# Attention probabilities divided before the transpose and used as the moving operand, pool weights folded into the output weights, and weight loads reordered

## The reference

```python
p = rmsnorm(h) @ w_in                         # q (8 heads x 64) | k, v (2 x 64) | u (512)
q, k = rope(q), rope(k)                       # first 16 dims of a head
s = q @ k.T / 8                               # keys: own and previous block of 128, masked to a window of 128
m = max(max(s), sink); e = exp(s - m)
a = (e / (sum(e) + exp(sink - m))) @ v
d[g] = windowed mean of u[g] - u[g]           # windows 2, 4, 8, 16; g = 0..3, 128 channels each
pm[g] = (d[g] @ pool_w[g]) * pool_scale[g]
h = h + concat(a, pm) @ w_out                 # 1024 x 1024
h = h + square(relu(rmsnorm(h) @ w_up)) @ w_down   # 1024 x 4096, 4096 x 1024
```

## Time and profile before

| | us |
|---|---|
| median of three runs (3076.12 to 3078.6) | 3076.51 |
| the profiled execution | 3078.81 |
| its span on the slowest core (core 7) | 3077.0 |
| spans of the eight cores | 3055.1 to 3077.0 |
| PE busy | 2822.4 |
| DVE, ACT, POOL busy | 1559.5, 1525.0, 181.1 |

### The profile page before, as it was taken

The page is one execution under the profiler, slowest core; times in us unless marked ns, Lnnn a source line. Parts: engine busy times, 40 slices in busy tenths (PEclk is TensorE's granted clock), DMA queues, the critical chain, the costliest instruction groups (busy, mean ns, idle before and its releaser), DMA issues.

```text
span 3077.0 us, 52361 instructions; the slowest of 8 cores (3055.1 to 3077.0 us)
## 1 busy us (share of the span) xinstructions
PE 2822.4 (92%) x17326; PEld 1462.9 (48%) x17326; DVE 1559.5 (51%) x3239; ACT 1525.0 (50%) x3827; POOL 181.1 (6%) x318
## 2 busy tenths in 40 slices
PE   1667899999999999999996777999999999999998
PEld 0334455545455555554453333545554554545445
DVE  1334454555465555554452444555556555555544
ACT  1434554545454555554552335555555555555544
POOL 0010000000000000000000100000000000000001
PEclk9888999999999999999998888999999999999999
DMA  9598125262534234245539972243433334242437
GB/s 200 110 191 200 61 91 178 97 193 97 162 123 144 111 125 150 98 172 146 165 113 196 205 175 81 85 166 109 141 122 110 151 108 164 86 165 103 159 112 246
DMA packets 105118, 431.69 MB, mean 140 GB/s; under 512 B 18700, under 2 KB 37100, under 8 KB 67896
## 3 DMA queue, kind: packets, MB, share of 16 engines
q0 software_dynamic: 76192, 314.30, 35.9%
q1 hardware_dynamic: 28664, 114.05, 10.8%
HBM read 404.04 MB, written 74.51 MB: 156 GB/s over the span
## 4 chain that ended last, share of the span: by engine, by line
PE 84%; DMA 9%; SPq 2%; issue 2%; DVE 2%; ACT 2%; DVEq 0%; ACTq 0%; POOLq 0%; POOL 0%
PE ps_all L1036 28%; PE ps_all L1054 28%; PE ps_all L588 10%; PE ps_all L978 7%; DMA s_wup<-w_up 3%; PE ps_all L548 2%; SPq L432 2%; PE ps_all L748 2%; PE ps_all L790 2%; DMA s_wdn<-dn_bf 2%; DMA s_wdn<-w_dn 1%; DMA s_h<-meta 1%; PE ps_all L749 1%; PE ps_all L750 1%; DVE s_xhat L541 1%
## 5 line engine op out<-in xcount | busy, mean ns | idle before, releaser
L1036 PE MATMUL ps_all<-s_xn2T,s_wup 128*128 128x512 bf16 (+2 forms) x4608 | 1029.9, 370 | 52.0 <-DMA s_wup<-w_up 41.0
L1054 PE MATMUL ps_all<-s_wdn,s_aT 128*128 128x512 bf16 x4288 | 1045.3, 382 | 21.8 <-DMA s_wdn<-w_dn 9.2
L1058 DVE TENSOR_TENSOR s_h<-s_h,ps_all 128x512 f32<-128x512 f32 x1072 | 735.4, 686 | 615.0 <-PE ps_all L1054 587.2
L1036 PEld LDWEIGHTS ps_all<-s_xn2T,s_wup 128*128 128x128 bf16 x4608 | 450.4, 99 | 514.7 <-issue 74.3
L1040 ACT ACTIVATE s_relu<-ps_all 128x512 f32<-128x512 f32 (+2 forms) x576 | 324.8, 567 | 674.2 <-PE ps_all L1036 672.6
L1054 PEld LDWEIGHTS ps_all<-s_wdn,s_aT 128*128 128x128 bf16 x4288 | 402.2, 98 | 452.5 <-issue 57.9
L1041 ACT ACTIVATE s_aT<-s_relu 128x512 bf16<-128x512 f32 (+2 forms) x576 | 344.5, 602 | 34.7 <-PE ps_all L1054 5.6
L588 PE MATMUL ps_all<-s_win,s_xnT 128*128 128x512 bf16 (+1 forms) x1632 | 315.5, 350 | 8.3 <-DVE s_xnT L553 5.7
L772 ACT ACTIVATE s_P<-ps_all,s_stat 128x256 bf16<-128x256 f32 x520 | 239.8, 478 | 117.0 <-DVE s_stat L762 116.0
L978 PE MATMUL ps_all<-s_wout,s_mixT 128*128 128x512 bf16 x1072 | 250.7, 385 | 1.9 <-ACT s_mixT L825 1.2
L588 PEld LDWEIGHTS ps_all<-s_win,s_xnT 128*128 128x128 bf16 x1632 | 161.2, 99 | 162.8 <-issue 22.2
(11 more groups left out here) (122 smaller groups left out, 2089.1 us busy)
## 6 DMA issues: line engine op xcount, KB each, us to landing
s_wup<-up_bf POOLq DMA_DIRECT2D x128, 1024.0 KB, 5.5
s_wdn<-dn_bf POOLq DMA_DIRECT2D x128, 1024.0 KB, 6.4
h_mid<-s_h SPq DMA_DIRECT2D x34, 512.0 KB, 6.8
s_h<-h_mid SPq DMA_DIRECT2D x34, 512.0 KB, 7.4
s_wup<-w_up POOLq DMA_DIRECT2D x16, 1024.0 KB, 28.0
s_wdn<-w_dn POOLq DMA_DIRECT2D x16, 1024.0 KB, 29.4
s_h<-x_p SPq DMA_DIRECT2D x32, 512.0 KB, 7.7
up_bf<-s_wup SPq DMA_DIRECT2D x16, 1024.0 KB, 10.2
```

Of the source, the lines that this page charges most:

```text
L1036: r = e.matmul(ps_t[bk][:, 0:n], lhsT=wup_t[s][:, k, fc * 128:(fc + 1) * 128], rhs=x2[:, k, 0:n], start=(k == 0), stop=(k == 7))
L1054: r = e.matmul(ps_t[db][:], lhsT=aT[:, fc, j * 128:(j + 1) * 128], rhs=wdn_t[s][:, fc, hf * 512:(hf + 1) * 512], start=(fc == 0), stop=(fc ...
L1058: dve(lambda e, hf=hf, db=db: e.tensor_tensor(out=h_t[hs][:, hf * 512:(hf + 1) * 512], in0=h_t[hs][:, hf * 512:(hf + 1) * 512], in1=ps_t[d ...
```

## The change

It has five parts.

1. P is multiplied by the reciprocals on DVE before its transpose. PV takes v as weights (64 columns) and P transposed as the moving operand (512 columns), the two kv heads in the two column halves of the array. The result is already transposed, so that the division, the transposes L822 and the small copies go.
2. `poolW` goes. Once per layer pool_w (given transposed) is scaled by pool_scale and multiplied into the lower half of w_out.
3. The sample tile moves from the second to the fourth group of each layer; its two kv halves are built side by side in one PSUM bank each, with two buffers for kc and vc.
4. Layer 0's groups 0 and 1 both read w_up and w_down as f32; the write-back is in group 1. In groups 2 to 6, after every second piece, one DRAM-to-DRAM cast on POOL prepares layer 1's weights (w_in, w_out, 16 pieces), which are then read as bf16 only.
5. At the start the first two tiles' rows go ahead of other loads, and masks, bmat, scales, sinks and the second gains wait for the first transposes, some x loads for those of an earlier tile. The planner gets one rate per queue. One relu buffer instead of two.

```diff
 MACROS = [
-    [[0, 1], [33, 2, 3, 4]] + [list(range(a, a + 4)) for a in range(5, 33, 4)],
+    [[0, 1], [2, 3, 4, 5], [6, 7, 8, 9], [10, 33, 11, 12]] + [list(range(a, a + 4)) for a in range(13, 33, 4)],
...
-DMA_BW = 300e3
+DMA_BW = {"pool": 330e3, "sp": 200e3, "act": 200e3}
...
-    r_t, r_b = sbn("relu", 2, [128, 512])
+    r_t, r_b = sbn("relu", 1, [128, 512])
...
     def load_x(l, ti, hs):
+        early = [first_pe[-2]] if l == 0 and 2 <= len(first_pe) < 8 else []
...
     def load_att_weights(l):
...
+            dma("pool", win_t[:].rearrange("p k n -> p (k n)"), win_d, reads=[win_db], writes=[win_b], sembuf=win_b)
...
+    converts = [(win_d.rearrange("p (k n) -> p k n", k=8), w_in[1].rearrange("(k p) n -> p k n", p=128), win_db),
+                (wout_d.rearrange("p (k n) -> p k n", k=8), w_out[1].rearrange("(k p) n -> p k n", p=128), wout_db)]
+    for p_ in range(NPIECE):
+        converts.append((up_d[1, p_].rearrange("p (k n) -> p k n", k=8), up_src(1, p_), up_db[1][p_]))
+        converts.append((dn_d[1, p_].rearrange("p (c n) -> p c n", c=4), dn_src(1, p_), dn_db[1][p_]))
+    def convert_next():
...
+        last = len(S.ops) - 1
+        while S.ops[last].eng != "pe":
+            last -= 1
+        out, in_, db = converts[i]
+        dma("pool", out, in_, writes=[db, cvt_b[i % 2]], sembuf=cvt_b[i % 2], after=[last])
...
-        if m == 0:
-            dma("pool", wup_t[s][:], w_up[l][:, p * 512:(p + 1) * 512].rearrange("(k p) n -> p k n", p=128),
-                writes=[wup_b[s]], sembuf=wup_b[s])
-            dma("sp", up_d[l, p], flat, reads=[wup_b[s]], writes=[up_db[l][p]], sembuf=wst_b[0][s])
+        if l == 0 and m < 2:
+            dma("pool", wup_t[s][:], up_src(l, p), writes=[wup_b[s]], sembuf=wup_b[s])
+            if m == 1:
+                dma("sp", up_d[l, p], flat, reads=[wup_b[s]], writes=[up_db[l][p]], sembuf=wst_b[0][s])
...
+    def fold_pool(l):
+        for g in range(4):
+            dve(lambda e, g=g: e.tensor_scalar(out=pw_t[:, g, :], in0=pw_t[:, g, :], scalar1=pscale_t[:, l * 4 + g:l * 4 + g + 1], scalar2=None, op0=ALU.mult),
+                [pw_b, pscale_b], [], pw=[fold_b[g]], cost=0.15)
...
+                for hf in range(2):
+                    r = e.matmul(ps_t[bk[hf]][:], lhsT=pw_t[:, g, :], rhs=wout_t[:, 4 + g, hf * 512:(hf + 1) * 512], start=True, stop=True)
...
+    def load_rest():
+        dma("sp", masks_t[:], masks_d, writes=[masks_b], after=[first_pe[0]], sembuf=masks_b)
...
-        act(lambda e: e.activation(out=d_t[:].rearrange("p g t -> p (g t)"), in_=ps_t[bdT][:], func=AF.Copy), [ps_b[bdT]], [d_b], cost=0.6)
-
-        def poolW(e):
...
+        act(lambda e: e.activation(out=mix[:, 4:8, :], in_=ps_t[bdT][:].rearrange("p (g t) -> p g t", g=4), func=AF.Copy),
+            [ps_b[bdT]], [], pw=[mixb], cost=0.6)
...
+                def normalise(e):
+                    r = None
+                    for hh in range(c0, c1):
+                        r = e.tensor_scalar(out=P[:, hh, :], in0=P[:, hh, :], scalar1=sT[:, 56 + hh:57 + hh], scalar2=None, op0=ALU.mult)
+                    return r
+                dve(normalise, [Bc, Pg[g]], [Pg[g]], cost=0.6)
...
-                    for h4 in range(4):
-                        hh = g * 4 + h4
-                        dst = ps_t[bpv][:, h4 * 64:(h4 + 1) * 64]
-                        e.matmul(dst, lhsT=PT[:, hh, 0, :], rhs=vu_prev[:, (hh % 2) * 64:(hh % 2 + 1) * 64], start=True, stop=False)
-                        r = e.matmul(dst, lhsT=PT[:, hh, 1, :], rhs=vu_own[:, (hh % 2) * 64:(hh % 2 + 1) * 64], start=False, stop=True)
+                    for hf, v in ((0, vu_prev), (1, vu_own)):
+                        for kv in range(2):
+                            r = e.matmul(ps_t[bpv][kv * 64:(kv + 1) * 64, :].rearrange("p (c t) -> p c t", c=4), lhsT=v[:, kv * 64:(kv + 1) * 64],
+                                         rhs=PT[:].rearrange("p (c k) f t -> p k f c t", k=2)[:, kv, hf], start=(hf == 0), stop=(hf == 1),
+                                         tile_position=(0, kv * 64))
...
-            def st_at(g, baT):
...
+            yield from sample_attention(l, par, qT, qTb, kT_own, kT_own_b, vu_own, vu_own_b, kcT_t, kcT_b, mix, mixb)
+        if l not in folded:
+            folded.add(l)
+            fold_pool(l)
...
             load_dn(q * NPIECE + p + 2)
+            if l == 0 and m >= 2 and p % 2 == 1:
+                convert_next()
...
+    load_x(0, 0, 0)
     dma("sp", ident_t[:], ident_d, writes=[ident_b], sembuf=ident_b)
+    load_x(0, 1, 1)
+    preloaded.update((0, 1))
+    load_att_weights(0)
     dma("sp", rope_t[:], rope_d, writes=[rope_b], sembuf=rope_b)
...
+        if q == 4:
+            dma("sp", lnf_t[:], lnf, writes=[lnf_b], sembuf=lnf_b, after=[first_pe[-1]])
```

More of the change, by code:

```diff
@@ L420, in build_program @@
     out_b = Buf("dram_out")
+    cvt_b = [Buf("cvt%d" % i) for i in range(2)]
+    win_db, wout_db = Buf("wind"), Buf("woutd")
     wst_b = [[Buf("wst%d_%d" % (k, i)) for i in range(2)] for k in range(2)]
@@ L465, in load_x @@
             seq, r = divmod(ti - 1, 16)
-            dma("sp", h_t[hs][:], x_p[seq, r * 128:(r + 1) * 128, :], writes=[h_b[hs]], sembuf=h_b[hs])
+            dma("sp", h_t[hs][:], x_p[seq, r * 128:(r + 1) * 128, :], writes=[h_b[hs]], sembuf=h_b[hs], after=early)
     def load_att_weights(l):
-        for gi in range(2):
-            dma("sp", g_t[gi][:], gbc[l, gi], writes=[g_b[gi]], sembuf=g_b[gi])
-        dma("pool", win_t[:], w_in[l].rearrange("(k p) n -> p k n", p=128), writes=[win_b], sembuf=win_b)
@@ L497, in load_dn @@
         flat = wdn_t[s][:].rearrange("p k n -> p (k n)")
-        if m == 0:
-            dma("pool", wdn_t[s][:], w_dn[l][p * 512:(p + 1) * 512, :].rearrange("(c p) n -> p c n", p=128),
-                writes=[wdn_b[s]], sembuf=wdn_b[s])
-            dma("sp", dn_d[l, p], flat, reads=[wdn_b[s]], writes=[dn_db[l][p]], sembuf=wst_b[1][s])
+        if l == 0 and m < 2:
+            dma("pool", wdn_t[s][:], dn_src(l, p), writes=[wdn_b[s]], sembuf=wdn_b[s])
+            if m == 1:
+                dma("sp", dn_d[l, p], flat, reads=[wdn_b[s]], writes=[dn_db[l][p]], sembuf=wst_b[1][s])
         else:
@@ L572, in att_tile @@
         norm_T(hs, 0, xnT, xnTb, par, bk[0])
+        if l == 0 and ti == 0:
+            load_rest()
         banks.give(*bk)
@@ L1162 @@
     shared = {
-        "meta": meta_tokens, "w_in": w_in, "w_out": w_out, "pool_w": pool_w, "w_up": w_up, "w_dn": w_down,
+        "meta": meta_tokens, "w_in": w_in, "w_out": w_out, "pool_w": f(pool_w.transpose(0, 1, 3, 2)), "w_up": w_up, "w_dn": w_down,
         "gbc": f(gbc), "pscale": f(psc), "sinkb": f(skb), "sinkc": f(skc), "lnf": f(lnfb),
```

350 lines of the change are left out of this document (198 added, 152 removed).

## The result

The changed kernel takes 2941.03 us (median of four runs, 2935.18 to 2947.96), the one before 3076.51 beside it: ratio 0.9559, 95% interval 0.9532 to 0.9586. It is 135 us faster; the forecast was 205, and 2941 lies 1 us outside the range. The profiled execution took 2935.18 us (span 2933.3), 143.6 less than the one before, where 204 were summed.

The account below looks back on a forecast made before the run. PE was taken to bound the steady stretches, and loading the start, the layer boundary and 1400 us. From 3078.8 us, -92 -107 -8 +8 -15 +10 = -204 gave 2874.8, as median 2872 us; range 2825 to 2940.

Parts of the forecast that it names:

- Startup, -92: Start through group 1: new load order and no write-back in group 0 win 122 us, 30 given back; bounds 122 and 60.
- I take 30 us of it as given back: Group 1, layer 0: casts, write-backs and tiles need 192 us of engine time for 162 us of PE work; costs 30 us.
- the 30 us of early waits: Before group 1's MLP: PE alone would allow 28 + 132 + about 30 us of early waits = 190.
- Boundary, -107: Where layer 1 takes over: bf16 weights remove casts and write-backs; 115 us lost there, 8 left; bounds 115 and 80.
- 1400 us, -8: At 1400 us w_in lands as bf16 in 7 us, not 21; the piece behind waits less: -8 of 13.
- The casts, +8: Eighteen DRAM-to-DRAM casts in layer 0's groups 2 to 6: hidden except at two cache-copy places, 8 us; bounds 0 and 90.
- The rival that made them the reason for "slower": DRAM-to-DRAM casts hold pieces behind them on their queue; gain lost at 11 us cost each, 3250 us at 55 each; chance 0.03.
- PE, -15: PV, transposes and pool product: -0.29 us per tile, -19 over 65 tiles, folding +4; bounds +13 and -28.
- The sample tile, +10: Moved to group 3 of each layer: PE waits if attention outlasts the covering MLP; 5 us per layer, bounds 0 and 30.
- the halves one after another: Rival: PV's two column halves do not overlap, 0.43 us more on 65 tiles, 28 us: 2900 us; chance 0.12.
- The loads keep up: Rival: in group 1 loads keep pace, startup -122 instead of -92, and the boundary clears fully: 2835 us; chance 0.17.
- Loading stays the bound: Rival: startup gains only 60 us and the casts cost 90: 2986 us; chance 0.10.

Follow-up runs that it names:

- early_casts: Changed kernel with w_up pieces 5, 6 and 7 of layer 0 cast DRAM to DRAM right behind the first four pieces, then read as bf16: 2921.89 us, ratio 0.9504.
- first_bf16: Changed kernel with layer 0's first group taking its sixteen weight pieces from a small bf16 constant instead of casting w_up and w_down: 2926.02 us, ratio 0.9496.
- no_fold: Changed kernel without folding pool_w and its scale into w_out: 2915.90 us, ratio 0.9484.
- no_convert: Changed kernel without the eighteen DRAM-to-DRAM casts; layer 1 reads layer 0's weights again: 2920.48 us, ratio 0.9496.
- casts_mid: Changed kernel with a group's four DRAM-to-DRAM casts issued after pieces 1, 2, 4 and 5 instead of 1, 3, 5 and 7: 2928.31 us, ratio 0.9482.
- half_steps: Changed kernel with only two of the sample tile's four steps, so half of its cache loads and small operations: 2949.87 us, ratio 0.9597.
- sample_back: Changed kernel with the sample tile back in the second group of each layer: 2997.59 us, ratio 0.9746.

## Why the prediction was wrong

Two terms carry the miss of 60 us: 42 stand in the two stretches that hide the sample tile (forecast +10 in sum, measured +52), 18 at the start.

- **Startup, -92.** Measured -74. Two errors in opposite directions. "MLP of group 1 starts at about 200 us" failed: it starts at 253. The sum took the casts as running without a pause to 189 us; with two buffers per weight they stop when the fourth piece has landed, until the first MLP at 105 (DMA share 0.08). From the first projection at 32 us to that MLP it is 73 us, for two tiles of attention, 26 us of work by the sum's own price, and the folding; the casts' sum left this path out, and the 30 us of early waits in PE's own were too few. early_casts shows the pause (17 to 19 us back by filling it), first_bf16 the casts (15 to 23 us of group 0's stretch, little of it kept in its profiled execution), no_fold 9 us before the first MLP for the folding. The other way, "I take 30 us of it as given back" failed too: group 1's phase took 157 us, not 190, write-backs included.
- **Boundary, -107.** Measured -106. Right, with its mechanism: clock 1.00, no wait for w_up or w_dn.
- **1400 us, -8.** Right in kind; the idle time there is gone altogether.
- **The casts, +8.** 20 by no_convert. The period of 20.3 us per piece was a mean; at a group's end it is 14. Whether placing them elsewhere gives some of it back is not shown (casts_mid). The rival that made them the reason for "slower" had the right place, but a cast costs about 1 us (20 in 18) and not 11. That it stays so is luck of the planned order, which the forecast put at nothing: in half_steps, where four casts go out just ahead of an urgent piece, each of these costs 8 to 21 us, and "a cast may take some 34 us before PE waits" fails there.
- **PE, -15.** The steady period gives -0.20 per tile, -13 in 65 tiles. The halves run together and the switch costs what the sample step showed. But without the folding, "+4" as work, the kernel is 23 us faster. 9 of them lie before the first MLP, where no earlier MLP hides it: the rows show a chain of scaling, matmuls and two copies between w_out's landing and the first output projection. The other 14 are open.
- **The sample tile, +10.** Measured +32 and +20 with the rest of those stretches; this is the largest error. "If that group's attention ends later than the MLP that covers it, PE waits" was the right mechanism with a size, 5 us per layer, taken from nothing in the trace. half_steps takes 16 us per layer off with half the steps. The second group of the kernel before had hidden most of the tile's long chain under its loading; sample_back shows that for layer 0 (12 us there against 21), not for layer 1, whose boundary has no such loading any more. What takes the pair's late core 10 to 16 us further in layer 0 is not settled: with layer 1's casts or half of the cache loads left out the two differ by 7 us at most, but all cores together still take 190 us there (188 in the changed kernel).
- **One core for all.** The late core of a pair costs up to 38 us against its neighbour, but the kernel before had late cores too, and the forecast started from its latest. From the fastest core before (3055.1) to the fastest after (2890.4) it is 165 us, 39 short of the 204. So the difference between the cores is no more than 21 of the 60.

Of the rivals, the halves one after another is out. "The loads keep up" was right about group 1 and wrong about the total; its 6.8 us per cast piece was too low (7.5 measured), and by the prediction's own figures 16 pieces at 6.8, with 59 us of write-backs and tiles, are 168 us of demand for 162, so not quite unbound either. "Loading stays the bound" was nearer, by time, than the forecast, but not by its mechanism at the boundary.

## What to carry to other kernels

Work out a load-bound stretch with the moments at which buffers come free, not with bytes over a rate: here the engines stood still for 29 us ahead of the stretch that they then bound. A tile with a long chain of dependent steps is cheapest where something else is waiting anyway; moving it into a full stretch costs what its chain outlasts the cover. In a queue served in order, put a long background transfer behind the urgent short one (read from the rows of four kernels, not tried by itself), and look at the shortest interval between urgent ones, not the mean.

## What the runs showed of the hardware

- Two neighbouring cores with the same program and the same transfers end up to 38 us apart (11 to 38 in the four runs of the changed kernel), and which of them is late changes from run to run. They part mostly where f32 is read: with group 0's casts gone its stretch is equal on all cores to within 1 us, where it ran from 134 to 154; with layer 1's casts gone the pairs differ by 10 to 23 us after group 0 and by 17 to 26 at the end, where with them 7 to 15 grew to 30 to 38. Why one of the two falls behind no run shows.
- Matmuls in two column halves of the array overlap in either order of issue: four of 512 columns start in two pairs 0.24 us apart, and the next full-width one 0.56 us after the first, where one after another they would need 0.86.
- A plain 1 MB bf16 load issued 1.2 us behind a DRAM-to-DRAM cast of the same size landed after 24.84 us (36 to 38 in two other places), against 6 on its own.
